# Attention of a two-layer encoder: scores in another order, three operand places, first scores ahead of the last query block, weighted values in two passes

## The reference

```
logits = q @ k.T * scale (+ decay, layer 0);  logits[masked] = -1e30
p = softmax(logits)
o = p @ v
...
x = x + concat_heads(o) @ w_o
```

## Time and profile before

| | |
|---|---|
| median of 3 runs | 1630.19 us (1629.72 to 1636.59) |
| the profiled execution | 1629.04 us, span 1627.2 us, mean granted clock 0.958 |
| busy, share of the span | PE 93%, DVE 66%, ACT 44%, POOL 25% |
| the chain that ended last | PE 67%, issue 8%, DVE 7%, ACT 3%, SP's queue 2%, DMA 2%, POOL 1% |
| matmuls of weighted values (L2121 to L2130) | 73.3 + 72.7 + 70.3 us (256 of each), 18.3 + 18.4 + 18.6 us (96 of each) |

### The profile page before, as it was taken

How to read it: one execution, slowest core, us unless ns; L and a number is a source line. 1 busy time by engine, 2 the same in 40 slices (tenths; PEclk the granted TensorE clock), 3 DMA queues, 4 the chain that set the end, 5 groups by cost and what they waited for, 6 DMA issues and landing times.

```text
span 1627.2 us, 30719 instructions
## 1 busy us (share of the span) xinstructions
PE 1510.8 (93%) x10741; PEld 1444.2 (89%) x10741; DVE 1076.0 (66%) x1969; ACT 715.8 (44%) x1478; POOL 399.5 (25%) x413
## 2 busy tenths in 40 slices
PE   8999938888999999999998897999998999999997
PEld 6788937788989999999998686999888999999997
DVE  5233226655987877877765235877598887778775
ACT  5232125654453343343334334777545334433434
POOL 0000034552432221221100002455243222222200
PEclk9999968989999999999999898999999999999998
DMA  8257675540123133133040537221012312322311
GB/s 287 91 158 187 154 201 137 141 122 27 53 78 104 52 103 103 52 103 102 27 146 11 179 137 210 83 65 33 27 52 79 104 55 100 103 84 71 103 52 59
DMA packets 129716, 164.13 MB, mean 101 GB/s; under 512 B 11936, under 2 KB 98912, under 8 KB 129648
## 3 DMA queue, kind: packets, MB, share of 16 engines
q1 hardware_dynamic: 129648, 163.23, 32.2%
HBM read 132.52 MB, written 30.68 MB: 100 GB/s over the span
## 4 chain that ended last, share of the span: by engine, by line
PE 67%; issue 8%; DVE 7%; ACT 3%; SPq 2%; DMA 2%; POOL 1%; ACTq 0%; POOLq 0%; DVEq 0%
PE ps L2222 26%; PE ps L2253 20%; PE ps L1847 10%; PE ps L2077 2%; PE ps L2121 2%; PE ps L2122 2%; PE ps L2123 2%; PE ps L2012 1%; SPq L548 1%; DVE nmx L1466 1%; DMA ql<-q_turned 1%; ACT pth L1043 1%; DVE wul L1325 1%; ACT prob L1033 1%; DVE wul L1573 1%
## 5 line engine op out<-in xcount | busy, mean ns | idle before, releaser
L1671 DVE TENSOR_TENSOR xT<-xT,ps 128x592 f32<-128x592 f32 (+1 forms) x256 | 194.9, 761 | 54.6 <-PE ps L2222 52.8
L1482 DVE TENSOR_TENSOR ptl<-ps,pth 128x256 fp32r<-128x256 f32 (+2 forms) x192 | 95.8, 501 | 116.2 <-ACT pth L1043 116.1
L2253 PE MATMUL ps<-bh,wuh 128*128 128x296 f32 (+1 forms) x512 | 152.8, 298 | 7.6 <-DVE wul L1573 5.0
L791 POOL TENSOR_TENSOR prob<-prob,rs 128x144 f32<-128x144 f32 (+4 forms) x160 | 119.1, 757 | 142.5 <-DVE rs L1472 141.6
L2253 PE MATMUL ps<-bl,wuh 128*128 128x296 f32 (+1 forms) x512 | 152.3, 298 | 0.0
L2253 PE MATMUL ps<-bh,wul 128*128 128x296 f32 (+1 forms) x512 | 152.0, 297 | 0.0
L858 POOL TENSOR_TENSOR ssum<-raw 128x512 f32<-128x512 f32 x32 | 49.0, 1533 | 291.7 <-DMA raw<-in_w_up 289.3
L1033 ACT ACTIVATE prob<-ps,nmx 128x144 f32<-128x144 f32 (+4 forms) x160 | 86.4, 540 | 59.2 <-DVE nmx L1466 58.4
L2222 PE MATMUL ps<-hh,dn2h 128*128 128x296 f32 (+1 forms) x512 | 111.0, 298 | 0.0
L2222 PE MATMUL ps<-hl,dn2h 128*128 128x296 f32 (+1 forms) x512 | 110.2, 296 | 0.0
L2222 PE MATMUL ps<-hh,dn2l 128*128 128x296 f32 (+1 forms) x512 | 110.2, 296 | 0.0
(11 more groups left out here) (282 smaller groups left out, 4710.5 us busy)
## 6 DMA issues: line engine op xcount, KB each, us to landing
raw<-in_w_up SPq DMA_DIRECT2D x32, 1024.0 KB, 7.2
raw<-in_w_down SPq DMA_DIRECT2D x32, 1024.0 KB, 5.1
raw<-in_w_in_a SPq DMA_DIRECT2D x12, 1024.0 KB, 9.0
kh<-k_turned SPq DMA_DIRECT2D x32, 212.0 KB
k_turned<-kst SPq DMA_DIRECT2D x48, 128.0 KB, 2.5
kv_mla<-stn SPq DMA_DIRECT2D x24, 256.0 KB, 2.2
q_turned<-qst SPq DMA_DIRECT2D x32, 148.0 KB, 2.6
qh<-q_turned SPq DMA_DIRECT2D x16, 296.0 KB
```

The source lines that it names most:

```text
L791: g.tensor_tensor(prob[c][0:rows, off:off + n], prob[c][0:rows, off:off + n], rs[0:rows, u:u + 1].to_broadcast([rows, n]), ALU.mult).then_ ...
L1482: v.tensor_tensor(dst, src, hi_part.bitcast(F32), ALU.subtract).then_inc(g_lo, 1)
L1671: v.tensor_tensor(a, a, two_banks(2 + m % 2, n), ALU.add).then_inc(x_ready if last else acc_done, 1)
L2253: i = te.matmul(ps[:, bank, 0:h], w[:, k, :], x, start=(u not in (3, 4, 6) and k == 0 and p == 0), stop=(k == 3 and p == 2), skip_group_ch ...
```

## The change

- Layer 0 gets an order of its own (`fox_step`) on TensorE, ScalarE and VectorE; layer 1 keeps the old one (now `mla_step`). TensorE: `p_turn 0, scores 0, p_turn 1, scores 1, scores 2, rest 1, rest 2, p_turn 2, rest 3, p_turn 3, scores 3, p_turn 4, scores 4, p_turn 5, weighted_v 0`.
- The last query block moves into head 0's step, behind scores 0 to 2. Query blocks 6 and 7 go to accumulator banks 4 to 7. The clearing of the margins of `prob` (`clear_prob`) moves behind the first three row maxima.
- A third place for a head's operands (`key_slot`), so that a head's loads wait for scores one head earlier. Heads 0 and 1 are loaded after block 3, the values of pairs 0 and 1 (into tiles of their own, `natv_first`) after block 4; the output weights stay after block 5. SyncE, GpSimd and TensorE have layer 0's heads written out in place of a loop.
- GpSimd normalises heads 0 and 1 ahead of the split of their pair's values.
- `vh` and `vl` become one tile `vlh`, low and high side by side. One matmul with its 128 columns gives low values by high probabilities (partitions 0 to 63) and high by high (64 to 127); a second with the 64 high columns adds high values by low probabilities. ScalarE copies the main part to `oh` and the rest to `corr`, VectorE subtracts into `rest_`, and GpSimd adds `rest_` and `corr` into `ol` once per pair (`add_parts`). This holds for both layers.

```diff
+        vlh = at("vlh", [P, 2, 7, 2, 2, HD], F32R, R_G + 23552)
+        corr, rest_ = sq[:, 0, :], sq[:, 1, :]
...
+        def q_banks(j):
+            return j % 2 if j < 6 else j - 4
+        def key_slot(h):
+            return (1, 0, 2)[h % 3]
...
 # SyncE
-                if j == 4:
+                if j == 3:
...
-                    fox_head(0, 0)
-                    fox_head(1, 1)
+                    fox_head(0, key_slot(0))
+                    fox_head(1, key_slot(1))
+                if j == 4:
+                    for i in range(4):
+                        sp.wait_ge(st_out[i], stored(i, N_BLK))
+                    fox_v(0, 0, natv_first[0])
+                    fox_v(1, 1, natv_first[1])
                 if j == 5:
                     load_wo(0)
-                if j == 6:
...
-                    sp.wait_ge(half_used, KVD0)
-                    fox_v(0, 0)
-                    fox_v(1, 1)
             for i in range(3):
                 sp.wait_ge(qt_out[i], 64 * len(range(i, PAIRS, 3)))
...
+            for h in range(2, HEADS):
+                if h == 2:
+                    sp.wait_ge(half_used, KVD0)
+                else:
+                    sp.wait_ge(s_ps, 5 * (h - 2))
+                fox_head(h, key_slot(h))
+                if h % 2 == 0 and h >= 4:
+                    sp.wait_ge(v_split, h // 2 - 1)
+                    fox_v(h // 2, h // 2 % 2, natv0[h // 2 % 2])
...
 # GpSimd
+                def add_parts(pair):
+                    pool.wait_ge(o_lo, pair * 2 + (H0 + 2))
+                    pool.wait_ge(o_corr, pair * 2 + (H0 + 2))
+                    g.tensor_tensor(ol[:, pair, :], rest_[:], corr[:], ALU.add).then_inc(o_sum, 1)
+                def head(h, c, pair=None):
+                    for u in range(4):
                         normalise(layer, h, c, u)
+                    if pair is not None:
+                        add_parts(pair)
+                    normalise(layer, h, c, 4)
...
                 for j in range(2):
+                    if layer == 0:
+                        head(j, j)
                     for part in range(3):
                         split_v(layer, j, j, 0, part)
...
 # ScalarE
                 def out(head, p, pair):
                     act.wait_ge(av_done, head + (H0 + 1))
-                    s.activation(oh[64 * p:64 * p + 64, pair, :], pf[0:HD, 3072:3072 + T],
-                                 ACT.Copy).then_inc(o_hi, 1)
+                    rows = slice(64 * p, 64 * p + 64)
+                    s.activation(oh[rows, pair, :], pf[HD:P, 3072:3072 + T], ACT.Copy).then_inc(o_hi, 1)
+                    if p == 0 and not (isinstance(pair, int) and pair == 0):
+                        act.wait_ge(o_sum, pair + (PAIRS * layer + 1))
+                    s.activation(corr[rows, :], pf[0:HD, 3072:3072 + T], ACT.Copy).then_inc(o_corr, 1)
+                def fox_step(h, c, pair, first=False, last=False):
+                    for u in range(2):
+                        if not first:
+                            turned(h, u)
+                        elif u == 0:
+                            act.wait_ge(half_used, KVD0 - 1)
+                        exp(h, c, u)
+                        if last and u == 0:
+                            wo_high(layer, 0)
+                    exp(h, c, 2)
+                    if first:
+                        query_hi(PAIRS - 1)
+                        exp(h, c, 3)
+                        exp(h, c, 4)
+                        return
+                    turned(h, 2)
+                    if not (isinstance(h, int) and h < 2):
+                        out(h - 2, c, pair - 1)
+                    turned(h, 3)
+                    exp(h, c, 3)
+                    turned(h, 4)
+                    exp(h, c, 4)
+                    turned(h, 5)
...
 # VectorE
+                    v.tensor_tensor(rest_[rows, :], pf[HD:P, 3072:3072 + T], oh[rows, pair, :].bitcast(F32),
                                     ALU.subtract).then_inc(o_lo, 1)
+                def fox_step(h, c, pair, first=False, last=False):
+                    if first:
+                        for u in range(3):
+                            row_max(h, u)
+                        clear_prob()
+                        query_lo(PAIRS - 1)
+                        recip(h, 0)
+                        recip(h, 1)
+                        row_max(h, 3)
+                        recip(h, 2)
+                        row_max(h, 4)
+                        recip(h, 3)
+                        return
+                    turned(h, 0)
+                    row_max(h, 0)
+                    recip(h - 1, 4)
+                    turned(h, 1)
+                    row_max(h, 1)
+                    recip(h, 0)
+                    row_max(h, 2)
+                    turned(h, 2)
+                    recip(h, 1)
+                    if not (isinstance(h, int) and h < 2):
+                        out(h - 2, c, pair - 1)
+                    if last:
+                        wo_low(layer, 0)
+                    turned(h, 3)
+                    row_max(h, 3)
+                    recip(h, 2)
+                    turned(h, 4)
+                    row_max(h, 4)
+                    turned(h, 5)
+                    recip(h, 3)
...
 # TensorE
-                            te.matmul(out, vh[0:rows, vs, t, d], pr_h, start=(b == 0), stop=False, skip_group_check=True)
-                            te.matmul(out, vh[0:rows, vs, t, d], pr_l, start=False, stop=False, skip_group_check=True)
-                            te.matmul(out, vl[0:rows, vs, t, d], pr_h, start=False, stop=(b == 1), skip_group_check=True)
+                            te.matmul(pf[:, cols], vlh[0:rows, vs, t, p, :, :].rearrange("p s d -> p (s d)"), pr_h,
+                                      start=(b == 0), stop=False, skip_group_check=True)
+                            te.matmul(pf[0:HD, cols], vlh[0:rows, vs, t, p, 1, :], pr_l, start=False, stop=(b == 1),
+                                      skip_group_check=True)
...
+                def fox_step(h, c, pair, nat, turn=0, first=False, last=False):
+                    if first:
+                        pe.wait_ge(kq_in[key_slot(0)], 80)
+                        for u in range(3):
+                            scores(h, c, u)
+                        query_block(PAIRS - 1)
+                        scores(h, c, 3)
+                        scores(h, c, 4)
+                        return
...
-                        pe.wait_ge(o_lo, H0 + HEADS - 2)
+                        pe.wait_ge(o_sum, PAIRS * layer + PAIRS)
...
-                pe.wait_ge(o_lo, H0 + HEADS)
+                pe.wait_ge(o_sum, PAIRS * (layer + 1) + 1)
                 wo_first(PAIRS - 1, PAIRS).then_inc(wo_ps, 1)
```

More of the change, by code:

```diff
@@ L1064, in step @@
                             out(h - 2, c, pair - 1)
-                        if layer == 1 and not last:
+                        if not last:
                             qk(h, u, 1 - c)
@@ L1457, in _ @@
                                 ALU.subtract).then_inc(qt_lo, 1)
+            for j in range(PAIRS - 1):
+                query_lo(j)
             def attention(layer):
@@ L1994, in _, with query_block @@
                     i.then_inc(F_ps, 1)
-            for j in range(PAIRS):
+            def query_block(j):
                 pc = 8 + 2 * (j // 4)
@@ L2016, in _ @@
                 i.then_inc(half_used if j % 4 == 3 else q_ps, 1)
+            for j in range(PAIRS - 1):
+                query_block(j)
             def attention(layer):
@@ L2136, in rest, with mla_step @@
                     weighted_v(h - 2, part, groups, pair, vs, p)
-                def step(h, c, pair, nat, turn=0, first=False, last=False):
+                def fox_step(h, c, pair, nat, turn=0, first=False, last=False):
[6 more added lines that the diff above has]
+                        scores(h, c, 4)
+                        return
+                    second = not (isinstance(h, int) and h < 2)
+                    p_turn(h, c, 0)
+                    pe.wait_ge(kq_in[key_slot(h)], 80 * (h // 3) + 80)
+                    scores(h, c, 0)
+                    p_turn(h, c, 1)
+                    scores(h, c, 1)
+                    scores(h, c, 2)
+                    if second:
+                        rest(h, 1, pair - 1, 1 - nat, c)
+                        rest(h, 2, pair - 1, 1 - nat, c)
+                    p_turn(h, c, 2)
+                    if second:
+                        rest(h, 3, pair - 1, 1 - nat, c)
+                    p_turn(h, c, 3)
+                    scores(h, c, 3)
+                    p_turn(h, c, 4)
+                    scores(h, c, 4)
+                    p_turn(h, c, 5)
+                    weighted_v(h - 1, 0, p_split(layer, h, 1) + G0, pair if c else pair - 1, nat if c else 1 - nat, 1 - c)
+                def mla_step(h, c, pair, nat, turn=0, first=False, last=False):
                     second = not (isinstance(h, int) and h < 2)
```

136 lines of the change are left out of this document (73 added, 63 removed).

## The result

| | before | after |
|---|---|---|
| median of 20 runs each | 1632.07 us (1626.74 to 1637.04) | 1636.28 us (1633.39 to 1641.46) |
| the profiled execution, span | 1627.2 us | 1634.2 us |
| busy PE, DVE, ACT, POOL | 93, 66, 44, 25% | 92, 66, 45, 26% |

The ratio is 1.0029, 95% interval 1.0017 to 1.0041: a loss of some 4 us, small but clear of the noise. The forecast of 1619 us, range 1606 to 1634, missed it, and the sign too.

A forecast was written before the change was run, and what follows sets the result against it. The prediction took a queue's order, value loads behind output weights on SyncE, as the first bound, then the ScalarE-VectorE chain. From 1629.04 us, -15.4 (start) +7.0 (steps) +0.8 (first end) -2.5 (second attention) = -10.1: 1619 us, range 1606 to 1634.

The forecast's parts named there:

- The start: Start of the first attention: the 23.41 us stall goes, head 2's maximum at 224.6 against 240.03, 15.4 us gained.
- 2.4 for the last to land: SyncE queue at the first attention's start: head 2's last operand load lands 2.4 us after issue, at 223.6.
- The steady heads: First attention's 13 steps: the new order lengthens each from 9.96 to 10.5 us, 7.0 us lost.
- its links: ScalarE and VectorE chain per step: unit 2's exponential -1.2, output copies +1.2, subtractions before maxima +2.1, hand-overs +0.1 us.
- In the first attention TensorE isn't on the chain, so this saves nothing there: First attention's weighted values: two passes save 0.72 us of TensorE work a head, but no time.
- Two passes: Weighted values: two matmuls per key group instead of three save 0.72 us a head, from the six 256-column groups.
- rival 4: Weighted values: weight-width changes drain TensorE, 22 a head at 0.16 us; 1665 us, chance 0.03.
- The second attention: Its loop: 0.72 us saved less 0.43 for the second copy, net 0.29 a head, 4.1 us gained over 14 heads.
- The ends: Ends of both attentions: GpSimd's addition costs +0.8 us each, plus 0.8 for low clock in the second.
- rival 1: Queue gives less back: weights issue in 19.03 us again, second attention gains nothing; 1627 us, chance 0.24.
- Rival 3: First attention: TensorE's clock stays at half and bounds the steps, deciding from 11.3 us a step; 1641 us, chance 0.12.
- The chance of a time under 1622 us: Whole kernel: more than 0.5% below the median, given 0.50 from forecast and rivals' spreads.

The follow-up runs named there:

- one_copy: Changed kernel without ScalarE's second copy of each head's output, GpSimd adding the rest to itself; 1633.47 us, ratio 1.0001 to the kernel before.
- last_three: wo_late_old_order with the last head of each attention in three passes of 64 columns and head 14's half pair added earlier; 1603.05 us, one run.
- wo_late: Changed kernel with the eight loads of the first attention's output weights moved behind head 15's loads; 1624.78 us, ratio 0.9955 to the kernel before.
- head2_early: wo_late_old_order with head 2's five loads ahead of the last query block's stores; 1602.80 us, one run.
- before_wo_mid: Kernel before with only the first attention's output weight loads moved behind head 9's operands and its pair's values; 1631.96 us, ratio 1.0001.
- best: wo_late_old_order plus the edits of head2_early and last_three, and the wait for all query stores behind head 3's loads; 1598.20 us, ratio 0.9794 to before.
- two_places: Changed kernel with the order of before in steps 1 to 15 and two operand places instead of three; 1626.46 us, one run.
- wo_late_old_order: wo_late's edit plus the order of before in the first attention's steps of heads 1 to 15; 1610.31 us, ratio 0.9855 to the kernel before.

## Why the prediction was wrong, step by step

**The start** is the step that failed: "2.4 for the last to land". The queue went nearly as followed: the weights issued from 200.42, not 194.7 (the values' issue ahead of them took 9.0 us, from 188.46 to 197.43, against 4.3 before), but in 12.2 us, not 15.4; head 2's loads began at 221.06, forecast 218.5. From the end of their issue to TensorE's first matmul it was 9.7 us, and the 2.4 had been taken from stores of 148 KB, the nearest row in the queue, not from loads of such operands. That is 7.3 of the 9.6 us that the start fell short; the 2.5 of the later issue, less 0.2 of shorter issue of these loads, are the rest. Of the 7.3, 3.7 are the loads' own (6.1 us alone, in before); the other 3.6 go with the loads of heads 3 and 4 right behind them, which the forecast left out: it followed the queue up to head 2's loads and no further. The weights cost by their issue alone; the delay is 9.6 us with them gone.

**The steady heads**: 10.5 was forecast, 10.72 measured, but two errors cancel in it in part. The order alone was counted at 9.9 and has 10.30 (which of its links holds the other 0.4 was not measured); the second copy was counted at 0.6 and has 0.35. The waits before the exponentials of units 3 and 4 came as said, 1.37 and 0.77 us. "In the first attention TensorE isn't on the chain, so this saves nothing there" holds for the new order, for which it was said (10.30 with three passes, 10.37 with two and one copy). What the prediction missed is that TensorE was on the chain of the old order: there two passes save 0.35 to 0.7 us a step (9.96 to 9.61 with two places, 10.16 to 9.48 with three), and the new order gave this away. Against the forecast's own baseline the loss is 9.9 us; against what the rest of the change would have had without the new order it is 16 (13 times 10.72 less 9.48).

**Two passes**: TensorE's rows in the second attention after (start, length), wide and narrow in turn:

```profile
1094.50 0.28 PE L2246 MATMUL ps<-pth,vlh 128*128 128x80 f32 x1
1094.61 0.23 PE L2248 MATMUL ps<-ptl,vlh 128*64 128x80 f32 x1
1094.67 0.28 PE L2246 MATMUL ps<-pth,vlh 128*128 128x80 f32 x1
...
1102.08 0.28 PE L2239 MATMUL ps<-pth,vlh 128*128 128x256 f32 x1
1102.19 0.28 PE L2241 MATMUL ps<-ptl,vlh 128*64 128x256 f32 x1
1102.31 0.28 PE L2239 MATMUL ps<-pth,vlh 128*128 128x256 f32 x1
```

A wide matmul with 256 columns takes 0.11 to 0.12 to the next start in such a row, one with 80 columns 0.11: the terms of the earlier trace rows held. A head's part 0, parts 1 and 2, and part 3 take 0.73, 1.21 and 0.51 us, where they took 0.92, 1.67 and 0.53: 0.67 less, 0.72 was forecast. The changes of width come 0.06 to 0.17 us after the start before them, 0.20 behind the first matmul of a head's part as before the change, and these sums leave no room for 0.16 us at each of 22 changes; rival 4 is out. The Trainium skill's rule that a change of mode drains TensorE (TensorEngine Tiling (Array Packing), Key Properties) shows no price here; that a change from 128 to 64 columns of weights is such a change of mode is not shown.

**The second attention**: -4.1 forecast, -4.1 measured, which is luck, for the reason is another. The sum was 0.72 less 0.43 for the copy. In fact the copy costs nothing (one_copy), and of TensorE's 0.67 only 0.26 a step arrive (9.79 to 9.53): TensorE, which was never idle there, now waits 0.5 to 0.65 us a step for the exponential of unit 2, at a granted clock still of 1.00. With one copy that wait is gone and the step is the same, so another loop sets it; which one was not settled. The 13 steps give 3.5 of the 4.1; seven more traces of the same code for this attention, from its first exponential to the last output copy, have 162.4 to 163.1 us, which is 2.0 to 2.7 less than before, where after has 161.1.

**The ends**: +0.8 each and 0.8 of clock were forecast; +2.6 and +3.0 came. The gap was right (3.07, forecast "about 3.3"), the addition was shorter (1.43, not 1.71). The gap is 1.5 us longer at either end; the rest goes with the clock, which was priced at 0.8 in one end and at nothing in the other. In the second it makes 1.5 in this run and 2.5 by last_three; in the first, 1.1, at a mean clock of 0.94 against 1.00 before.

**The rivals**: the queue gave less back, as rival 1 says, but by neither of its reasons: the weights issued in 12.2 us, not 19.03, and the second attention did gain; the loss came by landing. Rival 3's point of 11.3 us a step was not reached, so the forecast's limit held, but three smaller errors of one sign (start 9.6, steps 2.9, ends 3.2) did what that mechanism was to do. The chance of a time under 1622 us was added up wrongly: two thirds of 0.48, a tenth of 0.24 and 0.13 make 0.47, not 0.50.

## What to carry to other kernels

Price a transfer from the end of its issue to its first reader, by rows of the same kind of load, and look for such rows wherever a matmul waits for a DMA, even for 0.2 us; a store's landing in the same queue said nothing about it here. Count what is issued right behind it as well. An engine is off the loop only if nobody waits for it: read every engine's waits by releaser in the stretch before writing a saving down as hidden. A longer tail of hand-overs ahead of a dense stretch of matmuls should be priced with the stretch at low clock behind it, and the last item of a loop may take another path than the others.

## What the runs showed of the hardware

- Five loads of about 1.1 MB in all, those of one head, landed 6.1 us after the end of their issue when nothing else was moved (head 2 of before), and were in TensorE's hands 7.5 us after it with values behind them (head 7 of before), 9.0 to 10.4 with the loads of one or two more heads behind them (head 2 of after, wo_late and seven other runs, head 3 of head2_early), 11.0 right behind the weights (before_wo_mid, 308.38 to 319.40) and 12.8 behind another head's loads and stores (head 3 of best).
- Eight loads of 512 KB hold the queue for 11.95 to 19.03 us (11.95 in two_places, 12.22 in after, 17.25 in wo_late_old_order, 19.03 in before); what decides this was not tested.
- At the end of the second attention TensorE's granted clock fell to 0.62 for a stretch of 5 us behind a gap of 3.07 us and stayed at 1.00 behind one of 1.64; the 12 other traces agree.
